# Neighbourhood scores of two heads in 64 rows each, x through the weights' queue, and a new placing of stages and banks

## What is computed

```python
def even_proj(h, w_in, conv_w, gq, gk):
    bg, cg, xa, q, k, v = jnp.split(h @ w_in, 6, axis=-1)
    a = bg * short_conv(cg * xa, conv_w)
    q = rms_norm(q.reshape(B, L, NA_HEADS, NA_DH), gq)
    k = rms_norm(k.reshape(B, L, NA_HEADS, NA_DH), gk)
...
def na_latent(q, k, v, k_ctx, v_ctx, rpb):
    # 2-D neighbourhood (8 rows by 16 columns) on the latent grid plus 256 context keys, one softmax
    s_loc = jnp.einsum('brcqhd,brkcjhd->bhrcqkj', qg, kb).astype(jnp.float32) * scale
    s_loc = s_loc + bias[None].astype(jnp.float32)
    s_loc = jnp.where(valid[:, :, None, :], s_loc, NEG_INF)
    s_ctx = jnp.einsum('brcqhd,bmhd->bhrcqm', qg, k_ctx).astype(jnp.float32) * scale
    p = jax.nn.softmax(jnp.concatenate([s_loc, s_ctx], axis=-1), axis=-1)
...
for l in range(DEPTH):
    hp = modulate(yp, norm1_g[l], sh1p, sc1p)   # rms_norm(x, g) * (1 + scale) + shift
    hs = modulate(ys, norm1_g[l], sh1s, sc1s)
    # even layers: P takes dense attention inside each sequence, S takes na_latent
    yp = yp + g1p * mix_p
    ys = ys + g1s * mix_s
    yp = yp + g2p * sq_relu_mlp(modulate(yp, norm2_g[l], sh2p, sc2p), mlp_w1[l], mlp_w2[l])
    ys = ys + g2s * sq_relu_mlp(modulate(ys, norm2_g[l], sh2s, sc2s), mlp_w1[l], mlp_w2[l])
```

## Time and profile before

| what | us |
|---|---|
| runs shown, median of 3 | 2427.66 (2425.69 to 2431.66) |
| the profiled execution, its own time | 2432.97 |
| span of its slowest core (core 0) | 2431.3 |
| shortest span of a core (core 3) | 2401.9 |
| TensorE busy on core 0 | 2306.8, 95% of the span |
| DVE, ACT, POOL busy | 1163.8, 1162.2, 403.4 |

### The profile page before, as it was taken

One profiled execution on the slowest core, in us unless ns is written; L12 is line 12 of the kernel. 1 busy time (PEld: TensorE's weight loads), 2 busy tenths in 40 slices (PEclk: granted clock), 3 DMA queues, 4 the chain that ended last, 5 costly groups with the idle time before them and its releaser, 6 DMA issues.

```text
span 2431.3 us, 37746 instructions; the slowest of 8 cores (2401.9 to 2431.3 us)
## 1 busy us (share of the span) xinstructions
PE 2306.8 (95%) x13082; PEld 1120.9 (46%) x13082; DVE 1163.8 (48%) x1813; ACT 1162.2 (48%) x1953; POOL 403.4 (17%) x679
## 2 busy tenths in 40 slices
PE   3698899999999999999999999999999999999999
PEld 1354344445444544444444544444554454434444
DVE  1555453554446523364444645554444663335443
ACT  2564571533536467553234547643352656754111
POOL 3111211211102411121101211121210140000000
PEclk9799899999999999999999999999999999999999
DMA  9665899797543664569864588768865155452444
GB/s 191 109 121 107 165 168 165 130 167 121 99 75 53 116 107 79 96 114 180 133 113 87 80 143 164 142 120 149 139 115 85 27 91 90 70 112 48 75 78 113
DMA packets 95303, 275.53 MB, mean 113 GB/s; under 512 B 18704, under 2 KB 28304, under 8 KB 95120
## 3 DMA queue, kind: packets, MB, share of 16 engines
q0 software_dynamic: 74960, 238.88, 59.3%
q1 hardware_dynamic: 20160, 34.25, 4.7%
HBM read 500.27 MB, written 11.67 MB: 211 GB/s over the span
## 4 chain that ended last, share of the span: by engine, by line
PE 85%; DMA 8%; ACT 2%; issue 2%; DVE 1%; POOL 1%; DVEq 0%; ACTq 0%; POOLq 0%; SPq 0%
PE psall L721 85%; DMA WC<-ada_w 2%; DMA WC<-mlp_w 2%; DMA arena<-rpbx 1%; DMA arena<-ada_w 1%; DMA nav_out<-NT 1%; ACT arena L745 1%; DMA arena<-mlp_w 1%; DVE NT L767 1%; PE psall L729 0%; ACT RS L745 0%; POOL RT L756 0%; DVE arena L767 0%; ACT hT L745 0%; POOL arena L800 0%
## 5 line engine op out<-in xcount | busy, mean ns | idle before, releaser
L721 PE MATMUL psall<-arena 128*128 128x512 bf16 (+9 forms) x3896 | 805.5, 352 | 18.9 <-ACT arena L745 7.5
L745 ACT ACTIVATE arena<-psall 128x512 bf16<-128x512 f32 (+4 forms) x745 | 416.0, 578 | 670.8 <-PE psall L721 655.0
L721 PE MATMUL psall<-hT,WC 128*128 128x512 bf16 x2608 | 615.4, 385 | 21.9 <-ACT hT L745 12.9
L767 DVE SCALAR_TENSOR_TENSOR yT<-psall,mod,yT 128x512 f32<-128x512 f32 x480 | 359.2, 750 | 480.5 <-PE psall L721 479.6
L721 PEld LDWEIGHTS psall<-arena 128*128 128x128 bf16 (+1 forms) x3896 | 360.5, 98 | 414.7 <-issue 50.0
L721 PE MATMUL psall<-hT,arena 128*128 128x512 bf16 x2072 | 471.0, 380 | 0.5 <-DVE arena L767 0.3
L767 DVE SCALAR_TENSOR_TENSOR arena<-psall,arena 128x512 bf16<-128x512 f32 x384 | 264.6, 690 | 419.8 <-ACT arena L745 417.3
L721 PEld LDWEIGHTS psall<-hT,WC 128*128 128x128 bf16 x2608 | 254.1, 99 | 325.1 <-issue 49.5
L721 PE MATMUL psall<-arena,WC 128*128 128x512 bf16 x1408 | 327.2, 381 | 8.0 <-DMA WC<-mlp_w 6.4
L721 PEld LDWEIGHTS psall<-hT,arena 128*128 128x128 bf16 x2072 | 200.7, 98 | 234.1 <-issue 6.3
L721 PEld LDWEIGHTS psall<-arena,WC 128*128 128x128 bf16 x1408 | 135.7, 98 | 171.3 <-issue 17.6
(11 more groups left out here) (84 smaller groups left out, 1135.2 us busy)
## 6 DMA issues: line engine op xcount, KB each, us to landing
WC<-mlp_w POOLq DMA_DIRECT2D x128, 512.0 KB, 6.8
arena<-mlp_w POOLq DMA_DIRECT2D x128, 512.0 KB, 6.4
WC<-ada_w POOLq DMA_DIRECT2D x88, 512.0 KB, 7.6
WC<-even_w_in POOLq DMA_DIRECT2D x36, 512.0 KB, 8.1
arena<-rpbx SPq DMA_DIRECT2D x64, 240.0 KB, 5.4
WC<-even_w_out POOLq DMA_DIRECT2D x16, 512.0 KB, 7.2
WC<-odd_w_in POOLq DMA_DIRECT2D x16, 512.0 KB, 6.5
WC<-odd_w_out POOLq DMA_DIRECT2D x16, 512.0 KB, 6.2
```

The lines of the kernel that those rows point to most:

```text
L721: h.matmul(R(out), lhsT=R(lhsT), rhs=R(rhs), start=start, stop=stop, skip_group_check=skip))
L745: return lambda h: h.activation(out=R(out), in_=R(in_), func=func, **kw)
L767: P.add("dve", [lambda h: h.scalar_tensor_tensor(out=R(out), in0=R(in0), scalar=scalar, in1=R(in1), op0=op0, op1=op1)], reads, writes, vdu ...
```

## The change

1. **Scores.** `qTm` has one plane for two heads, no zeros. A piece of work takes both heads of a pair: one matmul with k and q in partitions 0 to 63, one in partitions 64 to 127, into two neighbouring banks, then one Exp, and for the grid one product, over both. The work is ordered by half image (8 grid rows, 512 tokens), 8 pieces in each: 2 of 512 columns a head, and on the grid 4 of 320 and 2 of 160. The v matmuls are the same 320- and 160-column ones as before, and 512 for the context. The cost model counts a pair at half (`par=2`).
2. **Start.** x goes through POOL's queue: block 0 ahead of the ada tiles, block 1 after the first tile of `even_w_in`, block 2 after the second. `norm` of block 0 first multiplies y by the root, into eight slots of its own, and applies scale and shift in one instruction afterwards.
3. **Placing.** `ZN` gives new zones of banks, `CF` new starts and ends of stages, `DMA_RATE` is 0.29e6 for 0.30e6, and the model's queue starts at 7 us.

```diff
-    DMA_RATE = 0.30e6
+    DMA_RATE = 0.29e6
...
-        dma_free = 0.0
+        dma_free = 7.0
...
+CF = dict(t0=1.9, cP0=33.6, cS0=82.0, hPa=-0.7, hPb=77.4, aBa=4.1, aBb=108.5, hS0=69.4, aS=(6.0, 13.2, 0.3, 0),
+          mPa=(0, -4.8, 5.9, 0), mPb=(0.9, 0.857, 0.886, 0.98), aA=0.598, mS=(4.9, 17.1, 0, 0),
+          aPa=(11.4, 0, 0, 7.0), aPb=(0.85, 0.804, 0.85, 0.82), aB=0.335)
+ZN = dict(conv=(0, 1, 2, 3, 4, 5, 6, 7), mP=((5, 6, 7), (6, 7), (5, 6, 7), (5, 6, 7)),
+          mS=((3, 4, 5, 6, 7), (4, 5, 6, 7), (2, 3, 4, 5, 6, 7), (3, 4, 5, 6, 7)), pool=(0, 1, 2, 3, 4, 5, 6, 7),
+          out=(3, 4, 5, 6, 7), u=(3, 4, 5, 6, 7), ada=(6, 7))
...
+            if early is not None:
+                tms = [Tl(P, early) for kc in range(8)]
+                for kc in range(8):
+                    f = lambda h, kc=kc: h.tensor_tensor(out=R(tms[kc][:]), in0=yT[:, kc, blk(tb)], in1=R(r), op=ALU.mult)
+                    P.add(("dve", "pool"), {"dve": [f], "pool": [f]}, [by[tb][kc], br], [tms[kc].b],
...
+                    fv = lambda h, kc=kc, o=o, sc=sc, sh=sh: h.tensor_scalar(out=o, in0=R(tms[kc][:]), scalar1=sc, scalar2=sh,
+                                                                           op0=ALU.mult, op1=ALU.add)
+                    fa = act_fn(o, tms[kc][:], AF.Identity, sh, sc)
...
-            qTm, bq_ = ar.take((128, 8, G.n), BF16, 8 * nb, "q")
+            qTm, bq_ = ar.take((128, 4, G.n), BF16, 4 * nb, "q")
...
-            Pr = ax.ring(4, (128, 512), BF16, "Pr" + n_)
+            Pr = ax.ring(3 if S else 2, (128, 1024), BF16, "Pr" + n_)
...
-                MEMSET(qv[64:128, :, 0, sl], 0.0, bq[k])
-                MEMSET(qv[0:64, :, 1, sl], 0.0, bq[k])
...
+            RG = [[(0, 0, 8, 0, 4), (1, 0, 8, 0, 0), (2, 4, 8, 1, 0)], [(1, 8, 12, 0, 8), (2, 8, 16, 1, 4), (3, 8, 16, 1, 0)]]
...
+                    DMA("sp", [(sg[:], rpbx[i, (2 * j + a) * 4 + u % 4])], [], [sg.b], None, key=hk - 3.0 + u * 0.01)
+                    ACT(tt_[:, a * 2 + sd, b * 480:b * 480 + 480], sg[:], AF.Exp, [sg.b], [tt_.b], key=hk - 1.9 + u * 0.05)
+                for hf in range(2):
+                    accs = [bank(AC2) for _ in range(2)]
+                    work = [("c", c, 0) for c in range(2)] + [("r", rg, b) for rg in RG[hf] for b in range(2)]
...
+                        s_ = Tl(P, P.banks, 2, [0, 2])
...
+                        MMG([(s_[:, a * 512:a * 512 + nr * 40].rearrange("p (r x) -> p r x", x=40), kT[hv[a], j, kvt(c, b) * 128:kvt(c, b) * 128 + 128],
+                              qs(a, j)[:, r0:r1, b * 24:b * 24 + 40], True, True) for a in range(2)],
+                            [bk[c // 2][j], bq[hf][j]], [s_.b], par=2)
+                        two = lambda x: x.rearrange("p (a x) -> p a x", a=2)[:, :, 0:nr * 40]
+                        ACT(two(p_[:]), two(s_[:]), AF.Exp, [s_.b], [p_.b])
...
-            xload(0, [])
+            xload(0)
             AR = Arena(4096, SZ).ring(8, (128, 8, 256), BF16, "WA")
-            wA = ada_part(0, "A", AR)
-            xload(1, [wA[3].b])
-            xload(2, [wA[5].b])
+            ada_part(0, "A", AR)
+            late.extend(xload(tb) for tb in (1, 2))
...
+        for x, w in zip(late, (0, 1, 5)):
+            x.key = first[w].key + 2e-7
```

More of the change, by code:

```diff
@@ L710, in isb, with MMG @@
             return True
-        def MMG(items, reads, writes, key=None):
+        def MMG(items, reads, writes, key=None, par=1):
             dur = 0.0
@@ L846, in ada_part @@
             n0 = 0 if part == "A" else 16
-            pt = bank(MI2 if l % 2 == 0 and part == "A" else MI)
+            pt = bank(ZN["ada"])
             for nt in tiles:
@@ L879, in rows, with norm @@
             return ap.rearrange("p (r b x) -> p r b x", r=8, b=2)
-        def norm(G, l, which, tb, key=None, zone=None):
+        def norm(G, l, which, tb, key=None, zone=None, early=None):
             blocks = G.name == "S" and which == 1 and l % 2 == 0
@@ L1202, in odd_attn @@
                 P.key = 14 + tt * 0.01
-                pt = bank(MM5)
+                pt = bank(ZN["u"])
                 for n in range(2):
@@ L1346, in qk_tile @@
                 if which == 0:
[L1347 to L1355, removed]
+                    if S:
+                        for b in range(2):
+                            STT(rows(qTm[:, j, sl])[:, :, b], grid(pt[:])[:, :, b], gqna_sb[:, i:i + 1],
+                                grid(r)[:, :, b], ALU.mult, ALU.mult, [pt.b, br, bsm], [bq[k][j]])
+                    else:
+                        STT(qTm[:, j, sl], pt[:], gqna_sb[:, i:i + 1], r, ALU.mult, ALU.mult, [pt.b, br, bsm], [bq[k][j]])
                 elif not S:
@@ L1411, in conv @@
                     sl = slice(k * 512, (k + 1) * 512)
-                    pt = bank(MI)
+                    pt = bank(ZN["conv"])
                     c0 = (j % 2) * 128
@@ L1417, in even_attn @@
             wbg = [None]
-            attT = qTm.rearrange("p (j two) t -> p two j t", two=2)[:, 0]
-            batt = [[bq[k][2 * j] for j in range(4)] for k in range(nb)]
+            attT, batt = qTm, bq
+            hv = [slice(0, 64), slice(64, 128)]
             if not S:
@@ L1456, in even_attn @@
+            for j in range(4):
+                hk = 10 + 2 * j
                 tt_ = Tl(P, TT_)
-                for u in range(4):
+                for u in range(8):
+                    a, sd, b = u // 4, u // 2 % 2, u % 2
                     sg = Tl(P, stg)
-                    DMA("sp", [(sg[:], rpbx[i, h * 4 + u])], [], [sg.b], None, key=hk - 2.0 + u * 0.01)
-                    ACT(tt_[:, u // 2, (u % 2) * 480:(u % 2) * 480 + 480], sg[:], AF.Exp, [sg.b], [tt_.b], key=hk - 0.9 + u * 0.05)
@@ L1494, in attn @@
+            out_proj(G, l, ewout[i], aT, baT, attT, batt, 20, ZN["out"])
         def attn(G, l):
@@ L1497, in build @@
         spans = {}
[L1498 removed]
+        late = []
         def group(name, fn, *args):
```

152 lines of the change are left out of this document (73 added, 79 removed).

## The result

| what | before | after |
|---|---|---|
| median of the runs compared, us | 2429.66 | 2403.01 (2402.03 to 2406.87) |
| ratio to before, 95% interval | | 0.9894 (0.9874 to 0.9914) |
| profiled execution: own time, slowest span, us | 2432.97, 2431.3 | 2403.16, 2401.6 (core 5) |

The kernel is 26 us faster by the ratio, 27 by the medians; the forecast was 29, to 2399. Where two kernels are compared, "by the ratios" is the difference of their ratios to before, times 2430 us.

A forecast was written before the change was run, and what follows sets the result against it. PE bounds the kernel, busy 2306.8 of 2431.3 us. Scores 12, start 9 and placing 8 sum to 29 us less, from 2427.66 to 2399 us; the forecast's own range is 2385 to 2412, over all cases 2370 to 2436.

The forecast's parts named there:

- Step 1, column time: Score matmuls of the even layers: if the two heads of a pair run at the same time, 21.2 us go.
- Step 2, switching: PE's 266 changes between 64 and 128 rows around score pairs: 0.035 us each, 9.3 us lost.
- My sign of being right: After a 64-row score pair, a group of 128-row matmuls starts 0.22 to 0.28 us later.
- The part as a whole: Scores, overlap less row changes: 12 us less, ends 21 less and 22 more.
- The first rival: The array empties at each change of rows, 0.164 to 0.250 us each; time 2433 to 2456, chance 0.13.
- Step 3, Exp and products at nothing: Exps and products of the scores: ACT loses some 13 us, all under PE's 95%, priced at nothing.
- Step 4, start: First 67 us: earlier first projection and gapless work, 9 us less, ends 3 and 17.
- Step 5, placing: PE's waits from 95.4 us on, under new banks and lists: 8 us less, ends 20 less and 12 more.
- No overlap: Each 64-row score matmul takes its full column time, so scores gain and lose nothing; 2411 us, chance 0.12.
- New waits from the placing: Even stages on two double banks: PE's waits grow by 10 rather than shrink by 8; 2417 us, chance 0.12.
- Clean: Changes of rows cost nothing and the placing gives more: 47 us less, 2381 us, chance 0.20.
- my signs: Over the whole run: PE busy near 2285 us, and idle below 60 from about 67 us on.

The follow-up runs named there:

- all 128 rows: The changed kernel with every score matmul reading k and q on all 128 partitions, so a score sums two heads; 2398.13 us, ratio 0.9861.
- old scores: The kernel before with the change's start and placing, keeping single heads, zero planes and one-bank Exps; 2398.72 and 2400.36 us, ratio 0.9881.
- scores only: The kernel before with the new scores alone (64 rows, shared Exp, half images), old start and placing; 2475.95 us, ratio 1.0197.
- placing only: The kernel before with the change's spans, zones and rate alone, old scores and old start; 2408.17 and 2412.62 us, ratio 0.9926.
- same half: The changed kernel with both heads' scores taken from partitions 0 to 63, same lists; 2421.31 us, ratio 0.9957.
- start only: The kernel before with x through POOL's queue and block 0's products ahead, old scores, zones and spans; 2425.28 us, ratio 0.9979.

## Why the prediction was right, and where it was not

**The total** was right, 29 for 26 us, and by luck: the scores were forecast to give 12 us and cost some 5, the placing was forecast to give 8 and gave 18 or more, and these two errors nearly cancelled.

**Step 1, column time.** Held: pairs of 512, 320 and 160 columns overlap wholly, 3 ns apart, 21.3 us as forecast.

**Step 2, switching.** This step failed. Its term was 266 x 0.035 = 9.3 us; a change costs 0.10 us, 26.6 in all. The 0.035 came from no row, only from an argument beside the 96-row one, and that row doesn't bear on it: 96 rows follow 128 without loss, 64 rows don't, not even when both matmuls use the same half. My sign of being right, a 128-row matmul 0.22 to 0.28 us behind the pair, was missed too: it is 0.32. The part as a whole is then +5 us and not -12; "all 128 rows" (5 to 8 us faster) and "old scores" (3 us faster) agree. The first rival, which I gave 0.13, was right that every change costs. Of its two terms the 0.164 us of tail isn't paid in full. The other, a weight load of 0.086 us that can't be made ahead, is what the trace shows (0.093 to 0.098), and it is near the whole price. The Trainium skill, "TensorEngine Tiling (Array Packing)", Key Properties, says that changing the mode drains TensorE. The trace agrees that a change costs, 0.10 us; since the profile models the ends of matmuls, it doesn't show whether the array was empty. 0.10 stays under the 0.144 us from which that rival would have decided the sign.

**Step 3, Exp and products at nothing.** Right under the new placing and wrong as a statement about the form. (ACT as a whole did not lose 13 us of busy time either: 1164.6 for 1162.2.) With the start new in both, the scores cost 0.0094 x 2430 = 23 us under the old placing, and 48 without the start, of which the switches explain 5. I named `ACT arena` as what would be waited for were the cover gone, 5.8 us; in "scores only" that wait is 12.0 us from 120 to 480, and PE's waits for `DVE arena`, 15.1 us, come on top.

**Step 4, start.** The chronology held: first projection 44.55 us (41.5), gapless from 65 (67), the ada tiles behind x block 0 in one queue only 2 to 3 us late, x blocks 1 and 2 at 49.5 and 58.9 us (49, 61). In idle time: 67 - 23.46 = 43.5 us up to 67 (forecast 44; 61.5 before, up to 95.4). The ends were 3 and 17, the term 9; the measured worth is 11 under the new placing and 5 under the old. I took less than the idle time because of slower matmuls. What the runs show is another reason that I didn't have: time won early is only kept if the stages behind move up. The stores' landing, which I counted into this step, fell from 12.5 to 3.6 us (median of four `nav_out`), and left the chain. Before, the first two of them were issued behind x block 2 in SP's queue, which landed at 74.6 us, and landed at 75.2 and 77.9; in "scores only" and "placing only", too, the first landed 0.7 us behind that block. The other two took 8.8 and 10.7 us with x already there, so the queue isn't all of it.

**Step 5, placing.** Mis-sized: 8 us forecast, 18 measured alone, 24 on top of the new start (0.0098) and 44 on top of start and new scores, the last two beyond my end of 20. I held that landings at a DMA share of 0.96 can't be moved by banks. They can by spans: weights were waited for 11.1 us, now 2.2, at a DMA share from 120 to 480 us of 0.84 against 0.82, and the runs part by their spans, 1.2 to 3.8 us with the new ones and 7.7 to 12.8 with the old. That the placing is worth more the more the other parts changed, I had no term for: I added the parts up.

**The other rivals.** No overlap: refuted by the 0.39 us of a pair and by "same half". New waits from the placing: PE's wait on `ACT arena` from 120 to 480 us is 5.1, not more; that for `arena L764` grew by 5 us, but PE's idle time there is 20.9 us against 21.5. Clean: a change isn't free. Of my signs, PE is busy for 2296.9 us and not near 2285, and idle from 67 us on for 61.2, just over 60.

**What stays open.** Which part of the new form (eight bias pieces through two slots, the Exp and product over two heads, the double banks, the half images) costs the 18 to 43 us beyond the switches under the old placing. The corner scores and placing without the start is missing. Whether a change costs its weight load, or a drain of about the same length, isn't separated.

## What to carry to other kernels

Two 64-row matmuls in separate halves overlap wholly, but each change between 64 and 128 rows costs 0.10 us. By that price (an estimate: 0.20 us against 0.216 / 512 us a column) a lone pair pays only above some 480 columns. Several pairs together would share the two changes, but no run here gained by it: four banks in one tile cost more than they saved. When one change bundles new code with a placing fitted to it, run the corners: here the placing carried most of the gain, and the new score code, without it, cost 23 to 48 us. Time won at the start of a planned kernel has to be given to the plan, or the next stages give it back.

## What the runs showed of the hardware that was not expected

- A change of rows, 128 to 64, costs 96 to 97 ns and back 93 to 104, with or without an overlap in the pair; 96 to 128 and back costs nothing: 215 ns from start to start at 512 columns, both ways (the earlier trace rows for one way).
- At such a change the weight load isn't made ahead of the matmul: it starts 4 ns before it, against 214 ns (at 512 columns) between matmuls of 128 rows or of 96 and 128.
- The granted clock in the first 120 us differs between kernels with nearly the same work: 0.97 in the change, 0.94 in "old scores", 0.84 in "start only". In "start only" the fall lies between 20 and 50 us, at 0.50 to 0.58 by tens of us, with PE busy for 1.7 to 5.5 us of each ten; in the change the clock is 1.00 there, with 1.9 to 5.5 us busy. The cause stays open, with one profiled execution of each.
